# A chunked recurrence scan: the triangular inverse's second orientation made by VectorE's block transposes instead of TensorE products

## The reference, cut to what matters

```python
def wkv_scan(r, v, decay, k, a_in, b_in, s0, reverse):
    def step(S, inp):
        rt, vt, wt, kt, at, bt = inp
        sa = jnp.einsum('bhij,bhj->bhi', S, at)
        S = S * wt[:, :, None, :] + sa[..., None] * bt[:, :, None, :] + vt[..., None] * kt[:, :, None, :]
        return S, jnp.einsum('bhij,bhj->bhi', S, rt)
...
```

## Time and profile before

| | |
|---|---|
| time, median of 3 runs | 3781.83 us (3774.82 to 3787.69) |
| span of the profiled execution | 3780.2 us |
| TensorE busy | 3524.4 us (93%) |
| VectorE busy | 2048.1 us (54%) |
| ScalarE busy | 698.6 us (18%) |
| GpSimd busy | 563.2 us (15%) |
| the scan stage, first to last matmul | about 2780 to 3438 us |

### The profile page before, as it was taken

The page is one execution under the profiler, slowest core; times in us unless marked ns, Lnnn a source line. Parts: engine busy times, 40 slices in busy tenths (PEclk is TensorE's granted clock), DMA queues, the critical chain, the costliest instruction groups (busy, mean ns, idle before and its releaser), DMA issues. The chain is left out here.

```text
span 3780.2 us, 60072 instructions
## 1 busy us (share of the span) xinstructions
PE 3524.4 (93%) x24875; PEld 1824.6 (48%) x24875; DVE 2048.1 (54%) x3270; ACT 698.6 (18%) x1383; POOL 563.2 (15%) x809
## 2 busy tenths in 40 slices
PE   6999998999989998999999999989998899888998
PEld 2354443334544445554444444543356676665443
DVE  1699983352356776557646566436533334344435
ACT  2100001122210111431100000335622222221000
POOL 0111111120000002000000110631113223332100
PEclk9999999999999999999999999999999999999999
DMA  9989995982244467335477686558854333335663
GB/s 366 333 302 330 344 347 208 330 326 77 73 183 175 175 239 263 106 126 202 166 257 255 227 326 229 167 190 273 266 158 152 107 104 112 105 100 181 240 223 111
DMA packets 362625, 799.01 MB, mean 211 GB/s; under 512 B 26630, under 2 KB 73790, under 8 KB 357746
## 3 DMA queue, kind: packets, MB, share of 16 engines
q1 hardware_dynamic: 259760, 459.54, 35.5%
q0 software_dynamic: 72992, 274.20, 20.1%
q10 hardware_dynamic: 29602, 61.42, 4.3%
HBM read 686.90 MB, written 108.18 MB: 210 GB/s over the span
## 5 line engine op out<-in xcount | busy, mean ns | idle before, releaser
L1228 PE MATMUL gemm_a_g_ps<-store_w,turned 128*128 128x512 f32 (+1 forms) x1152 | 457.6, 560 | 2.7 <-PEq L108 2.7
L759 DVE SCALAR_TENSOR_TENSOR pmods_acc<-pmods_w,cond,pmods_acc 128x512 f32<-128x512 f32 x540 | 384.4, 749 | 23.6 <-issue 0.5
L1228 PEld LDWEIGHTS gemm_a_g_ps<-store_w,turned 128*128 128x128 f32 x1152 | 209.4, 191 | 250.3 <-issue 250.3
L3084 PE MATMUL scan_g_ps<-store_w,turned 64*64 64x512 f32 x2048 | 288.1, 610 | 10.5 <-DVE outlet_stage L3098 6.8
L1228 PE MATMUL att_a_g_ps<-store_w,turned 128*128 128x512 f32 x512 | 240.2, 599 | 6.9 <-ACT outlet_stage L2812 4.2
L1228 PE MATMUL feat_g_ps<-store_w,turned 128*128 128x512 f32 x384 | 181.9, 622 | 14.6 <-ACT outlet_stage L2240 12.4
L1275 PE MATMUL out_c_g_ps<-store_w,turned 128*128 128x512 f32 x384 | 167.6, 592 | 0.0
L1228 PE MATMUL tail_g_ps<-store_w,tail_branch_t 128*128 128x512 f32 x384 | 165.7, 592 | 0.9 <-ACT tail_branch_t L3913 0.9
L3449 DVE TENSOR_TENSOR scan_tm<-scan_tm,scan_ps 128x256 f32<-128x256 f32 x128 | 53.8, 421 | 168.8 <-PE scan_ps L3337 168.6
L1228 PEld LDWEIGHTS att_a_g_ps<-store_w,turned 128*128 128x128 f32 x512 | 91.5, 191 | 100.0 <-issue 93.4
L3337 PE MATMUL scan_ps<-scan_tmt,scan_y 64*64 64x64 f32 x2560 | 118.9, 223 | 14.2 <-issue 10.7
(11 more groups left out here) (577 smaller groups left out, 5934.0 us busy)
## 6 DMA issues: line engine op xcount, KB each, us to landing
store_w<-in_w_in SPq DMA_DIRECT2D x160, 1024.0 KB, 7.9
pmods_w<-in_w_mod POOLq DMA_DIRECT2D x40, 2048.0 KB, 13.2
store_w<-in_a_w_in SPq DMA_DIRECT2D x48, 1024.0 KB, 10.9
store_w<-in_c_w_in SPq DMA_DIRECT2D x40, 1024.0 KB, 8.4
first_mods_w<-in_w_mod SPq DMA_DIRECT2D x32, 1024.0 KB, 14.3
store_w<-in_a_w_out SPq DMA_DIRECT2D x32, 1024.0 KB, 6.2
scan_raw<-s_feat SPq DMA_DIRECT2D x112, 256.0 KB, 4.5
s_feat<-feat_o POOLq DMA_DIRECT2D x16, 1536.0 KB, 7.9
```

Source lines behind the costliest of these rows:

```text
L759: v.scalar_tensor_tensor(a, src, x, a, ALU.mult, ALU.add)
L1228: mm = pe.matmul(to, lhs, self.store.slot[i % self.store.NS][:, k, :width], start=first, stop=last)
L3084: mm = pe.matmul(self.ps[r][halves[o], :], self.act_tile(k, tb)[halves[r], halves[o]], self.store.slot[i % self.store.NS][halves[r], k % 4 ...
```

## The change

TensorE no longer computes A itself nor the update of T. VectorE makes T from the transpose by transposing 32x32 blocks. Up to level 4 the blocks that are inverted are at most 32 wide, so all of T lies in diagonal 32x32 blocks (the others are zero), and turning each block in place is the whole transpose. Level 5 needs no T.

- `products` loses the eight matmuls of `A_` for each direction. Levels 1 to 4 lose the eight of `update_t`.
- The identity is added on VectorE to the result of `half k` (stage `y k`: `y1` = product + I). So `level k` gives the new transpose itself, not an update. ScalarE's copy of `half k` goes.
- `t k` on VectorE is now `turn`: one block transpose of the even heads (128 partitions x 128) and two of the odd heads (64 partitions x 128 each, onto the other chunk's partitions), from PSUM to `tm`, and a drain. `tt k` moves to ScalarE, which copies the new transpose to `tmt` after VectorE has turned it.
- At the start of a round `t0` on VectorE adds the identity to `tmt` and turns it. GpSimd's two additions for each direction go, and so does `at_`'s fourth operation.

The diff, cut to its core:

```diff
@@ -3153,9 +3153,10 @@
...
                 + ["tz", "outer", "chain1"] + ["y"] * lat + ["chain2"],
-                "dve": ["ft", "at", "ak"] + ["rk"] * lat + [f"{a}{k}" for k in levels for a in ("t", "tt")][:-2] + [f"tt{N_LEVELS}"] + ["pm", "m1", "m2"],
-                "act": ["ft", "av"] + [f"half{k}" for k in levels] + ["tz", "outer"] + ["y"] * lat,
-                "pool": ["eye"] + [f"lt{k}" for k in levels] + ["dg"],
+                "dve": ["ft", "at", "ak", "t0"] + ["rk"] * lat + [f"{a}{k}" for k in levels for a in ("y", "t")][:-1]
+                + ["pm", "m1", "m2"],
+                "act": ["ft", "av"] + [f"tt{k}" for k in levels] + ["tz", "outer"] + ["y"] * lat,
+                "pool": [f"lt{k}" for k in levels] + ["dg"],
@@ -3206,9 +3207,9 @@
...
             return ps[d][:, b, :].rearrange("p (j c) -> p j c", c=P)
-        STRICT, UPTO, FIRST, FIRST_T = 0, 1, 2, N_LEVELS + 3
+        STRICT, UPTO, FIRST = 0, 1, 2
         PACE, N_PIECES = ("products", "level1", "level3", "level5"), 4
-        AT, A_, AK, RB, RK = 0, 1, 2, 3, 2
+        AT, AK, RB, RK = 0, 2, 3, 2
@@ -3264,13 +3265,12 @@
...
-            def inner(d, o, x, y, cross=False):
+            def inner(d, o, x, y):
...
                     for h, to in ((hp, 0), (hp + 1, 1), (hp, 1), (hp + 1, 0)):
-                        c = 1 - to if cross and h % 2 else to
-                        mm = pe.matmul(product(d, o)[chunks[to], h % 2, h // 2, :], head(ft[d], h, x)[:, chunks[c]],
-                                       head(ft[d], h, y)[:, chunks[c]], start=True, stop=True)
+                        mm = pe.matmul(product(d, o)[chunks[to], h % 2, h // 2, :], head(ft[d], h, x)[:, chunks[to]],
+                                       head(ft[d], h, y)[:, chunks[to]], start=True, stop=True)
@@ -3287,7 +3287,6 @@
...
                 inner(d, AT, 1, 0)
-                inner(d, A_, 0, 1, cross=True)
@@ -3309,10 +3308,7 @@
...
                     after(pe, d, "pool", g, s, f"lt{k}")
-                    if k > 1:
-                        after(pe, d, "dve", g, s, f"t{k - 1}")
-                    elif lat:
-                        after(pe, d, "dve", g, s, "rk")
+                    after(pe, d, "dve", g, s, "rk" if lat and k == 1 else f"t{k - 1}")
@@ -3322,35 +3318,16 @@
...
                 def f(d, g, s, lat):
-                    after(pe, d, "act", g, s, f"half{k}")
-                    if k > 1:
-                        after(pe, d, "dve", g, s, f"tt{k - 1}")
-
-                    def update_t(h):
-                        for c in range(2):
-                            to = chunks[1 - c if h % 2 else c]
-                            pe.matmul(crossed(d, 0, 0)[to, h % 2, h // 2, :], tmt[d][chunks[c], h, :],
-                                      y1[d][chunks[c], h, :], start=True, stop=True)
-
-                    def update_tt(h):
+                    after(pe, d, "dve", g, s, f"y{k}")
+                    after(pe, d, "act", g, s, f"tt{k - 1}" if k > 1 else "av")
+                    for h in range(HG):
                         for c in chunks:
-                            mm = pe.matmul(quarter(d, 2, 1)[c, h, :], y1[d][c, h, :], tmt[d][c, h, :],
-                                           start=True, stop=True)
-                        return mm
-                    if k < N_LEVELS:
-                        for h in range(0, HG, 2):
-                            update_t(h)
-                            update_t(h + 1)
-                            update_tt(h)
-                            mm = update_tt(h + 1)
-                    else:
-                        for h in range(HG):
-                            mm = update_tt(h)
+                            mm = pe.matmul(quarter(d, 2, 1)[c, h, :], y1[d][c, h, :], tmt[d][c, h, :], start=True, stop=True)
...
             def tz_(d, g, s, lat):
-                after(pe, d, "dve", g, s, f"tt{N_LEVELS}")
+                after(pe, d, "act", g, s, f"tt{N_LEVELS}")
@@ -3415,6 +3392,7 @@
...
             v.wait_ge(tables, 64)
+            eye = eye2[:, :].unsqueeze(1).broadcast_to([P, HG, HD])
@@ -3422,14 +3400,27 @@
...
                 after(v, d, "pe", g, s, "products")
-                a_t, a = product(d, AT), product(d, A_)
+                a_t = product(d, AT)
                 strict = masks[:, d, STRICT, :].unsqueeze(1).broadcast_to([P, HG // 2, HD])
+                v.tensor_tensor(by_parity(tmt[d]), a_t, mask_by_parity(d, FIRST), ALU.mult)
...
                 v.tensor_tensor(by_parity(at[d])[:, 1, :, :], quarter(d, 2, 0)[:, 0:HG // 2, :], strict, ALU.mult)
-                v.tensor_tensor(by_parity(tmt[d]), a_t, mask_by_parity(d, FIRST), ALU.mult)
-                v.tensor_tensor(by_parity(tm[d]), a, mask_by_parity(d, FIRST_T), ALU.mult)
...
                 v.sem_inc(dve_done[d], 1)
+
+            def turn(d, src):
+
+                even, odd = by_parity(tm[d])[:, 0, :, :], by_parity(tm[d])[:, 1, :, :]
+                v.transpose(even, by_parity(src)[:, 0, :, :])
+                for c in range(2):
+                    v.transpose(odd[chunks[1 - c]], by_parity(src)[chunks[c], 1, :, :])
+                v.drain()
+                v.sem_inc(dve_done[d], 1)
+
+            def t0(d, g, s, lat):
+                v.tensor_tensor(tmt[d][:, :, :], tmt[d][:, :, :], eye, ALU.add)
+                v.drain()
+                turn(d, tmt[d][:, :, :])
@@ -3443,16 +3434,16 @@
...
+            def y_(k):
+                def f(d, g, s, lat):
+                    after(v, d, "pe", g, s, f"half{k}")
+                    v.tensor_tensor(by_parity(y1[d]), crossed(d, 0, 1), by_parity(eye), ALU.add).then_inc(dve_done[d], 1)
+                return f
+
...
                     after(v, d, "pe", g, s, f"level{k}")
-                    v.tensor_tensor(by_parity(tm[d]), by_parity(tm[d]), crossed(d, 0, 0), ALU.add).then_inc(dve_done[d], 1)
-                return f
-
-            def tt_(k):
-                def f(d, g, s, lat):
-                    after(v, d, "pe", g, s, f"level{k}")
-                    v.tensor_tensor(tmt[d][:, :, :], tmt[d][:, :, :], quarter(d, 2, 1), ALU.add).then_inc(dve_done[d], 1)
+                    turn(d, quarter(d, 2, 1))
@@ -3470,11 +3461,11 @@
...
                 return f
-            run = {"ft": ft_, "at": at_, "ak": ak, "rk": rk, "pm": pm_, "m1": m_(0), "m2": m_(1)}
+            run = {"ft": ft_, "at": at_, "ak": ak, "t0": t0, "rk": rk, "pm": pm_, "m1": m_(0), "m2": m_(1)}
             for k in levels:
-                run[f"t{k}"], run[f"tt{k}"] = t_(k), tt_(k)
-            made_by = {"ft": "turned", "at": "products", "ak": "products", "pm": "outer", "m1": "chain1", "m2": "chain2"}
-            made_by.update({f"{a}{k}": f"level{k}" for k in levels for a in ("t", "tt")})
+                run[f"y{k}"], run[f"t{k}"] = y_(k), t_(k)
+            made_by = {"ft": "turned", "at": "products", "ak": "products", "t0": "products", "pm": "outer", "m1": "chain1", "m2": "chain2"}
+            made_by.update({f"{a}{k}": f"{b}{k}" for k in levels for a, b in (("y", "half"), ("t", "level"))})
@@ -3484,8 +3475,8 @@
...
                 names = stages("dve", steps[s][2])
-                order = [("ft", 0), ("ft", 1), ("at", 0), ("ak", 0), ("at", 1), ("ak", 1)]
-                order += [(stage, d) for stage in names[3:] for d in range(2)]
+                order = [("ft", 0), ("ft", 1), ("at", 0), ("ak", 0), ("at", 1), ("ak", 1), ("t0", 0), ("t0", 1)]
+                order += [(stage, d) for stage in names[4:] for d in range(2)]
@@ -3496,9 +3487,11 @@
...
         def _(act):
-            def copies(name_of_product, pairs):
+            def copies(name_of_product, pairs, turned_first=None):
...
                     after(act, d, "pe", g, s, name_of_product)
+                    if turned_first:
+                        after(act, d, "dve", g, s, turned_first)
@@ -3519,13 +3512,14 @@
...
                 "y": y}
+
             for k in levels:
-                run[f"half{k}"] = copies(f"half{k}", lambda d, lat, x: [(by_parity(y1[d]), crossed(d, 0, 1))])
+                run[f"tt{k}"] = copies(f"level{k}", lambda d, lat, x: [(tmt[d][:, :, :], quarter(d, 2, 1))], f"t{k}" if k < N_LEVELS else None)
...
                     for d in range(2):
-                        while t < tiles_by(max(0, visit_of[(g, s, "turned" if stage == "ft" else stage, d)] - 6)):
+                        while t < tiles_by(max(0, visit_of[(g, s, {"ft": "turned"}.get(stage, stage.replace("tt", "level")), d)] - 6)):
@@ -3540,8 +3534,6 @@
...
                     after(pool, d, "dve", g, s, "at")
-                    pool.tensor_tensor(tm[d][:, :, :], tm[d][:, :, :], eye, ALU.add)
-                    pool.tensor_tensor(tmt[d][:, :, :], tmt[d][:, :, :], eye, ALU.add).then_inc(pool_done[d], 1)
```

## The result

The changed kernel takes 3790.59 us against 3781.98 for the kernel before: a ratio of 1.0026, with an interval from 1.0018 to 1.0035. It is 9 us slower, and at the edge of what a measurement of this kernel tells from no change. The forecast of 3771 us had the wrong sign, and the time lies within its range. The profiled execution has a span of 3784.7 us, 4.5 us more than before's 3780.2.

A forecast was written before the change was run, and what follows sets the result against it. TensorE, busy for 93% of the span, was taken as the bound, with the loop partly bound by hops. Loop +6, starts -1, output tiles -3, stalls +8: 10 us won, so 3771 us, range 3742 to 3806.

The forecast's parts named there:

- What TensorE saves: In levels 1 to 4 and `A_`: TensorE freed after 0.91 us a level; ceiling 35.7 us if no hop shows.
- VectorE's hop: In the levels: the first result of a lone level reaches VectorE 0.69 us after the level's start.
- The turn: On VectorE between level and half: three block transposes and a drain, taken as 0.88 us.
- If a transpose is like them: Block transposes in a turn assumed to overlap like 128-column operations: starts 0.21 us apart, 0.29 long, 0.84 with the drain.
- The argument for 0.88: In a turn: a 32x32 block must fill before leaving, and 32 columns cost only 0.03 to 0.04 us.
- the same formulas: Loop periods from VectorE's in-order queue: 1.16 + 2T, or 1.84 + 2T with a unit after the half; T a turn's time.
- The 6 us won in the loop: Over 64 level steps: 10.2 us won with a unit after the level only, 4.2 lost after the half only.
- rival 1: Transposes of a turn on VectorE don't overlap, 1.00 us or more: slower, 3791 us, 3825 at 1.21; chance 0.34.
- The start of a round: VectorE takes over the identities and two turns, `A_`'s 0.47 us isn't won: 1 us lost in all 16 rounds.
- the sums' price among the levels: Output tiles' 1.37 us sums in VectorE's queue: five or six fall amid levels, 0.6 us more each, 3 us lost.
- The stalls: TensorE's unexplained stops, about 55 us in 16 rounds, taken to shrink with 16% fewer records: 8 us won.
- periods of 2.92 and 3.60: Expected loop periods in us: 2.92 with a unit after the level only, 3.60 with one after the half.

The follow-up runs named there:

- the start alone: The kernel before with `A_` and GpSimd's identities removed and `t0` on VectorE, the levels' update of T kept: 3786.27 us, ratio 1.0028.
- the first experiment: The changed kernel with one transpose of all four heads for three in each turn, odd heads' inverse left out: 3739.59 us, ratio 0.9889 to before.

## Why the prediction was wrong

**What TensorE saves** held. A level of levels 1 to 4 frees TensorE for the unit behind it after 0.86 us (3147.45 to 3148.31), and 0.98 in the next step (3150.82 to 3151.80), for 0.91 reckoned. VectorE's hop is 0.70 (3147.45 to 3148.15) for 0.69.

**The turn** is the step that failed. "If a transpose is like them" took T from additions, whose starts are closer than their length. In the turn the starts are 0.33 apart for a length of 0.32: T = 1.10 for 0.88. The argument for 0.88, that columns are cheap, was right on columns (one transpose of 256 takes 0.45) and said nothing on the fixed part, which comes three times. At 1.10 the same formulas give 3.36 and 4.04 for the measured 3.37, 4.05 and 4.08. The 6 us won in the loop became 23.3 lost. This is rival 1. It was priced at T = 1.00 with 3791; its price at 1.10 would have been some 3807. That the measured time is just 3791 is luck: the turn cost more than rival 1 had it, and the stalls gave back more than the forecast had.

The trace of the kernel before held rows that would have warned. The operations of the earlier trace rows all start on partition 0. Where an addition of the same scan works on the other half of the partitions than the one before it, it doesn't overlap it. Two additions each, first from one half to the other, then on the same partitions:

```profile
2830.47 0.87 DVE L3470 TENSOR_TENSOR scan_m<-scan_ps,scan_m 64x256 f32<-64x256 f32 x2
3133.56 0.75 DVE L3455 TENSOR_TENSOR scan_tmt<-scan_tmt,scan_ps 128x256 f32<-128x256 f32 x2
```

An addition takes 0.42 in both. The first pair starts 0.03 us behind its predecessor's end (28 such pairs in the scan, all 0.03), the second pair 0.08 ahead of it. In a turn each transpose starts to read or to write on other partitions than the one before, the unused fourth too, and no run has two transposes on the same partitions without a drain between them. So that the three stand in line is shown; whether it is because they are transposes or because they change partitions is not.

The Trainium skill ("VectorE: DVE Perf Modes", section "The DRAIN you can't avoid") says that an operation waits until the pipe has emptied, and in the same place that one that is not held starts earlier, which the prediction left out. The transposes of a turn agree with the first (0.33 apart for 0.32 long), the additions on the same partitions with the second (0.21 for 0.29). Its 311 ns for a 128x128 transpose in bf16 (section "The three transpose paths") is what fp32 takes here too: 317 ns from PSUM.

**The start of a round** was put at 1 us lost in 16; it was 15.7. With T at 1.10 each round loses two times 0.22 more than reckoned, 7 us, and so 8 in all; the regular starts lost 8.5. Some 5.5 us more come in two rounds, where the tile's sum stands behind `t0`. The prediction looked for the sums' price among the levels (3 us lost) and didn't ask which work `t0` itself was put ahead of: a sum that TensorE waits for. The last 1.7 us I can't place for certain; the eight additions of `t0` in latent rounds that take 0.81 us beside a mask, some 3 us in all, were not reckoned and are the nearest row. That the start alone measures 1.0028 puts a number on this part.

**The stalls** were sized by their count alone, 8 us won. The gaps over 0.6 us shrank by 29.6 us in the scan, and the steps ran 31.7 us closer to their regular periods (40.3 us above them before, 8.6 after). So the regular loss of 23.3 us in the levels turned into a gain of 8.4. The kept matmuls brought 14.0 us of gaps and 17 us of time back, but they also filled 25 us of waits; the waits added to the kernel before took 23.1 us of gaps away with the instructions unchanged. So waits are a part of it, and the number of instructions by itself is not shown to be. Some of it stands beside a lower clock: before, 5 steps touch a stretch at half of it and run 11.8 us over, gaps included; after, 2 steps and 0.8 us. Taken together the rows would fit a TensorE that uses instructions faster than they arrive (a regular step with a unit after the level only has 64 + 32 + 8 matmul records and as many weight loads in 3.24 us before, 64 a microsecond; 61 with the removed matmuls kept, 52 in the first experiment, 43 in the kernel after), but no row shows the supply, and of before's 25 gaps four stand at a DMA share of 1.04 to 1.07 and 18 at 0.26 or less. The cause stays open.

**Sum.** Reckoned: 6 - 1 - 3 + 8 = 10 us won. By the profiled executions, one of each kernel, the levels won 10.6, the starts lost 15.7, the rest won 2.3: 2.9 lost in the scan of the 4.5 by which the span grew. The medians say 9; single executions differ by some microseconds in their stalls.

**Signs named beforehand.** The idle time of the loop is ended by VectorE (58.0 us), as said; half 1 waits for `t0` or `rk` (10.0 us), as said; periods of 2.92 and 3.60 didn't come, nor did starts 0.2 apart. Of the signs named for rival 1, no transpose is over 0.35 us long, and the level (L3325) waits little; the line that waits for the turn is the half (L3314), as the working had it.

One statement ahead of the prediction is wrong: of the odd heads only `tm`, `at` and `lt` lie on the other chunk's partitions; `y1` lies on its own.

## What to carry to other kernels

Work moved from a busy engine to an idle one is priced by the instructions that it becomes in the loop's chain of hops, not by its columns or by busy shares: three transposes cost 1.10 us where one of the same elements cost 0.57. A length of overlap read from one kind of row holds for operations that lie as those do, on the same partitions here. Before a layout is kept that spares the busy engine, price what it costs the engine that must turn the data; here giving up the layout made the version that beats both, though most of its lead over the kernel before is in disturbances that no row explains. Where an operation is put early in a queue, look for what is now behind it, and expect that idle time on TensorE won or lost is partly exchanged with its unexplained stalls.

## What the runs showed of the hardware

- Block transposes of fp32 on VectorE: 317 ns for 128x128 and 314 for 64x128 from PSUM, 450 for 128x256; starts 0.33 us apart, where each reads or writes from other partitions than the one before.
- VectorE's additions on the same partitions start 0.08 us ahead of the predecessor's end (0.29 long, 0.21 apart); those that move to the other half of the partitions start 0.03 us behind it.
- VectorE's additions out of SBUF and GpSimd's masks lengthen each other: `t0`'s addition of 128x256 took up to 0.81 us for 0.42, the unused additions 0.79 in the mean for 0.42, and the masks 0.90 to 0.94 for 0.72. Beside transposes from PSUM the masks stayed at 0.72.
- 32 records of 64x64 matmuls (a half of both directions) hold TensorE for 0.47 us over four quadrants and for 0.83 over two.
- TensorE has idle gaps of up to 3.4 us that nothing in the profile ends: 39.1 us in the scan before, 9.5 after, 23.5 with the removed matmuls kept and 33 us of waits for the turn in place of 58, 16.0 with the instructions of before and more waits.
- With four transposes in each turn the granted clock was 0.94 in the scan for 0.98, and steps that touch a stretch at 0.50 of full speed took 20.8 us more than undisturbed ones.
